# Eight rows of w_gu to a partition, loaded up to 8 MB at a time, with the residual banks holding alternate groups of four columns

## The reference

```
logits = x @ w_router + b_router            # (256, 32); top 4, softmax over the four -> gates
for e in 32 experts:
    h  = x @ w_gu[e] + b_gu[e]              # w_gu[e] is 1024 x 2048: 8 MB
    hg, hu = min(h[:, :1024], 7), clip(h[:, 1024:], -7, 7)
    y  = ((hu + 1) * hg * sigmoid(1.702 * hg)) @ w_down[e] + b_down[e]     # w_down[e] is 1024 x 1024: 4 MB
    out += gate[:, e] * y
```

## Time and profile before

| | |
|---|---|
| median of 3 runs | 1048.63 us |
| the profiled execution's own time | 1049.05 us |
| its span, from first to last instruction | 1047.2 us |
| TensorE matmuls busy | 989.3 us, 94% of the span |
| VectorE busy | 235.0 us, 22% |
| ScalarE busy | 143.3 us, 14% |
| moved by the DMA engines | 421.74 MB, 403 GB/s over the span |
| mean granted TensorE clock | 0.994 of full speed |

### The profile page before, as it was taken

How to read it: one execution, slowest core, us unless ns; L and a number is a source line. 1 busy time by engine, 2 the same in 40 slices (tenths; PEclk the granted TensorE clock), 3 DMA queues, 4 the chain that set the end, 5 groups by cost and what they waited for, 6 DMA issues and landing times.

```text
span 1047.2 us, 12857 instructions
## 1 busy us (share of the span) xinstructions
PE 989.3 (94%) x5782; PEld 413.5 (39%) x5783; DVE 235.0 (22%) x531; ACT 143.3 (14%) x273; POOL 15.9 (2%) x27
## 2 busy tenths in 40 slices
PE   8999999999999999999999999998999889899996
PEld 7875543433333333333333333333333333333332
DVE  3995341111111111111111111101111111011121
ACT  5144320000010101010100010000101000000103
POOL 4000000000000000000000000000000000000001
PEclk9999999999999999999999999999999999999999
DMA  9995489999999999999999999999999999999994
GB/s 307 387 416 196 181 322 409 427 412 427 433 429 431 432 427 426 434 427 432 428 433 427 434 425 437 423 439 423 435 425 433 426 434 429 431 430 430 423 424 165
DMA packets 31220, 421.74 MB, mean 403 GB/s; under 512 B 3791, under 2 KB 8187, under 8 KB 13628
## 3 DMA queue, kind: packets, MB, share of 16 engines
q1 hardware_dynamic: 29612, 420.57, 95.3%
q10 hardware_dynamic: 1552, 0.33, 0.2%
HBM read 419.82 MB, written 1.05 MB: 402 GB/s over the span
## 4 chain that ended last, share of the span: by engine, by line
PE 60%; DMA 25%; DVE 11%; ACT 2%; issue 1%; SPq 0%; POOLq 0%; POOL 0%; DVEq 0%
PE work L1085 52%; DMA ring<-in_w_gu 24%; PE resid L1085 5%; DVE main L821 4%; DVE main L1004 2%; PE work L1405 2%; DVE main L1001 2%; DVE main L997 2%; ACT main L672 1%; DMA ring<-in_w_in 1%; PE work L1201 0%; PE work L1297 0%; DVE main L828 0%; DVE ring L800 0%; DVE ring L831 0%
## 5 line engine op out<-in xcount | busy, mean ns | idle before, releaser
L1085 PE MATMUL work<-ring,main 128*64 128x512 f32 (+1 forms) x3096 | 683.6, 593 | 20.1 <-DMA ring<-in_w_gu 17.8
L1085 PEld LDWEIGHTS work<-ring,main 128*64 128x64 f32 (+1 forms) x3096 | 224.2, 138 | 466.4 <-issue 435.4
L997 DVE TENSOR_SCALAR main<-work 128x512 f32<-128x512 f32 x32 | 22.1, 692 | 738.3 <-PE work L1085 738.3
L672 ACT ACTIVATE main<-main 128x512 f32<-128x512 f32 x32 | 20.2, 631 | 504.0 <-DVE main L997 504.0
L1085 PE MATMUL work<-ring 128*128 128x256 f32 (+2 forms) x308 | 71.9, 403 | 2.1 <-DVE ring L774 0.9
L1085 PE MATMUL resid<-main 128*128 128x512 f32 x128 | 67.6, 613 | 0.9 <-DVE main L1056 0.9
L686 ACT ACTIVATE main<-work 64x512 f32<-64x512 f32 x63 | 37.3, 592 | 215.0 <-PE work L1085 214.6
L1085 PEld LDWEIGHTS work<-ring 128*128 128x128 f32 (+1 forms) x308 | 55.6, 186 | 16.8 <-issue 8.3
L1085 PE MATMUL work<-bgu_rows,ident 128*64 128x512 f32 x256 | 60.8, 594 | 0.0
L1085 PEld LDWEIGHTS work<-select,main 128*128 128x128 bf16 x1536 | 46.6, 98 | 26.2 <-issue 25.2
L1085 PE MATMUL work<-select,main 128*128 128x64 bf16 x1536 | 50.4, 193 | 0.1
(11 more groups left out here) (182 smaller groups left out, 256.0 us busy)
## 6 DMA issues: line engine op xcount, KB each, us to landing
ring<-in_w_gu SPq DMA_DIRECT2D x39, 4096.0 KB, 39.7
ring<-in_w_down SPq DMA_DIRECT2D x20, 4096.0 KB, 39.9
ring<-in_w_gu SPq DMA_DIRECT2D x30, 2048.0 KB, 15.4
ring<-in_w_gu SPq DMA_DIRECT2D x9, 3072.0 KB, 38.2
ring<-in_w_down SPq DMA_DIRECT2D x13, 2048.0 KB, 14.5
ring<-in_w_gu SPq DMA_DIRECT2D x13, 1024.0 KB, 33.2
ring<-in_w_down SPq DMA_DIRECT2D x4, 3072.0 KB, 36.1
ring<-in_w_down SPq DMA_DIRECT2D x9, 1024.0 KB, 28.0
```

The lines of the kernel that those rows point to most:

```text
L672: nc.scalar.activation(sig_h, gate_h, ACT.Sigmoid, scale=SWIGLU_ALPHA).then_inc(sig_ready, 1)
L997: V.tensor_scalar(gate_h, work[:, GATE_BANK, :], SWIGLU_LIMIT, None, ALU.min).then_inc(gate_clamped, 1)
L1085: return nc.tensor.matmul(out_, lhsT, rhs, start=start, stop=stop, skip_group_check=True)
```

## The change

w_gu is laid out with eight neighbouring rows to a partition, one in each up unit, and `UP_GROUP` becomes 8: an expert's eight up units come in one load of 8 MB that reads 64 KB in one run for each partition. Such loads are used from expert 12 on (`HALVES_UP_TO`) to expert 29. Experts before it keep the load sizes that they had (2 units in the first six, then 4), as do experts 30 and 31, but they too have the new row order: a load of 2 units reads 16 KB out of every 64 KB, and one of 4 units reads 32 KB out of every 64 KB. Where a load crosses the end of the ring it is still cut in two.

The rest follows from the row order. A residual bank now holds, of every eight columns, the first four (h = 0) or the last four (h = 1). `project`, `add_bdown` and `down` read their moving operand in groups of four columns with gaps, as `up` did before, and write 512 neighbouring elements. ScalarE copies x into the banks in this order, `gained` reads the final gain and writes the result in groups of four. The gain `norm_ffn_g` comes as one row and is turned by eight small transposes in place of four. Two waits on `o_gained` now ask for both halves, since each multiplication writes into both halves of the result.

```
-    UP_GROUP, DOWN_GROUP = 4, 4
+    UP_GROUP, DOWN_GROUP = 8, 4
-    FINE_UP_TO, FINE_FROM = UNITS * 6, UNITS * (E - 2)
+    FINE_UP_TO, HALVES_UP_TO, FINE_FROM = UNITS * 6, UNITS * 12, UNITS * (E - 2)
-                sizes.append(UP_GROUP if n % UNITS < UP_UNITS else DOWN_GROUP)
+                sizes.append((UP_GROUP if n >= HALVES_UP_TO else UP_GROUP // 2) if n % UNITS < UP_UNITS else DOWN_GROUP)
-        gain_rows = unit(2)[0:2, P:P + 4 * P]
+        gain_rows = unit(2)[0:1, P:P + D]
+        def columns_of(view, h):
+            return view.rearrange("p (j h b) -> p h j b", h=2, b=4)[:, h, :, :]
+        def as_columns(view):
+            return view.rearrange("p (j b) -> p j b", b=4)
-                    g, b = u // 4, u % 4
-                    return w_gu[e, 4 * P * g:4 * P * (g + 1), :].rearrange("(p b) n -> p b n", b=4)[:, b:b + size, :]
+                    return w_gu[e, :, :].rearrange("(p b) n -> p b n", b=KB)[:, u:u + size, :]
...
-                pool.wait_ge(o_gained, h + 1)
+                pool.wait_ge(o_gained, 2)
...
-                nc.scalar.activation(resid[:, t, :], x_sb[:, t, :], ACT.Copy).then_inc(x_added, 1)
+                nc.scalar.activation(resid[:, t, :].rearrange("p (h j b) -> p h j b", h=2, b=4),
+                                     x_sb[:, t, :].rearrange("p (j h b) -> p h j b", h=2, b=4), ACT.Copy).then_inc(x_added, 1)
...
-                V.tensor_tensor(result[:, t, half], resid[:, t, half], final_gain[:, half], ALU.mult).then_inc(o_gained, 1)
+                V.tensor_tensor(columns_of(result[:, t, :], h), as_columns(resid[:, t, half]), columns_of(final_gain, h), ALU.mult)\
+                    .then_inc(o_gained, 1)
...
-                    dve.wait_ge(o_gained, 2 * t + 1)
+                    dve.wait_ge(o_gained, HALVES)
...
-            for b in range(4):
-                last = nc.tensor.transpose(work[:, 3, G_FFN + b:G_FFN + KB:4], gain_rows[:, b:4 * P:4], ident[0:2, 0:2])
+            for b in range(KB):
+                last = nc.tensor.transpose(work[:, 3, G_FFN + b:G_FFN + b + 1], gain_rows[:, b:D:KB], ident[0:1, 0:1])
...
-                    last = mm(resid[:, t, h * HALF:(h + 1) * HALF],
+                    last = mm(as_columns(resid[:, t, h * HALF:(h + 1) * HALF]),
-                              piece(name)[:, kb, h * HALF:(h + 1) * HALF], False, False)
+                              columns_of(piece(name)[:, kb, :], h), False, False)
...
-                            last = mm(work[CAP * h:CAP * (h + 1), UP_BANK if is_last else OUT_BANK, :], lhsT, row[:, h * HALF:(h + 1) * HALF],
+                            last = mm(as_columns(work[CAP * h:CAP * (h + 1), UP_BANK if is_last else OUT_BANK, :]), lhsT, columns_of(row, h),
```

More of the change, by code:

```diff
@@ L186, in hybrid_layer @@
         vec_rows = unit(2)[0:28, 0:P]
-        gain_rows = unit(2)[0:2, P:P + 4 * P]
-        dw_rows = unit(2)[0:TAPS, 5 * P:5 * P + D_CONV]
+        gain_rows = unit(2)[0:1, P:P + D]
+        dw_rows = unit(2)[0:TAPS, P + D:P + D + D_CONV]
         fg = unit(16)[0:HEADS, 0:6 * SEQ].rearrange("p (n t) -> p n t", n=6)
@@ L350, in _ @@
                 at += n
-            sp.dma_start(gain_rows, norm_ffn_g.rearrange("(m q) -> m q", q=4 * P)).then_inc(vecs_in, 16)
+            sp.dma_start(gain_rows, norm_ffn_g.rearrange("(m q) -> m q", q=D)).then_inc(vecs_in, 16)
             sp.dma_start(dw_rows, w_dw).then_inc(dw_in, 16)
@@ L522, in _ @@
             for t in range(TB):
-                nc.scalar.activation(resid[:, t, :], x_sb[:, t, :], ACT.Copy).then_inc(x_added, 1)
-            act.dma_start(wr_sb[:, :, :].rearrange("p (m b) n -> p m (b n)", b=4), w_router.rearrange("(m p b) n -> p m (b n)", p=P, b=4)).then_inc(router_in, 16)
+                nc.scalar.activation(resid[:, t, :].rearrange("p (h j b) -> p h j b", h=2, b=4),
+                                     x_sb[:, t, :].rearrange("p (j h b) -> p h j b", h=2, b=4), ACT.Copy).then_inc(x_added, 1)
+            act.dma_start(wr_sb[:, :, :].rearrange("p b n -> p (b n)"), w_router.rearrange("(p b) n -> p (b n)", b=KB)).then_inc(router_in, 16)
             act.dma_start(br_row[:, :], b_router.partition_broadcast(P)).then_inc(router_in, 16)
@@ L1362, in add_bdown @@
                     for h in range(2):
-                        mm(resid[:, t, h * HALF:(h + 1) * HALF], gates_t[:, t * P:(t + 1) * P], bdown_sb[:, h * HALF:(h + 1) * HALF], False, False)
+                        mm(as_columns(resid[:, t, h * HALF:(h + 1) * HALF]), gates_t[:, t * P:(t + 1) * P], columns_of(bdown_sb, h), False, False)
             def scatter(buffer, t, h, rows=P):
```

## The result

The changed kernel takes 1055.72 us (median of 5 runs, 1055.2 to 1058.64) against 1049.58 us (5 runs): a ratio of 1.0061, with a 95% interval of 1.0047 to 1.0074, or +6.4 us. The forecast of 1051.7 had the sign and was short by 4.0 us. Of these, 0.95 is the kernel before, whose median was 1048.63 when the forecast was made. As a difference, +3.1 was forecast, and +6.1 (by the medians) to +6.4 (by the ratio) was measured; rival A, at +7.0, is nearer.

The account below looks back on a forecast made before the run. The prediction took w_gu[29]'s landing, paced by the DMA, plus 83.9 us behind it as the bound. Terms +6.8 - 3.9 + 0 + 0.2 = +3.1 us on 1048.63 gave 1051.7 us; 8-in-10 range 1048.5 to 1057.0.

Parts of the forecast that it names:

- rival A: DMA loads of w_gu: the large packets save nothing, so the time is 1055.6 us; chance 0.20.
- What bounds the kernel: End of the kernel: landing of the last unit of w_gu[29] plus 83.9 us of TensorE and closing work.
- Point 1: Expert 29's ups: the 8 MB load is waited for whole, 64 instructions behind its landing instead of 32, +6.81 us.
- Point 2: DMA queue: waiting for eight free slots does not run it dry, cost 0; 1 us left for a late load.
- the margin of 7 us: DMA queue at expert 12, the tightest place: at 436 it still has 7 us of work.
- the limit of 0.98: DMA share in 430 to 1000: falling below this anywhere would show the claim of no dry queue wrong.
- Point 3: Experts 12 to 29: one transfer fewer each, 18 x 0.22 = 3.9 us by which w_gu[29] lands earlier.
- The prediction's own sign: Trace of the changed kernel: ten experts take 292.2 us instead of 294.4 if fewer transfers save time.
- the line through two stretches: DMA in 440 to 560 and 963 to 1000: 36.3 ps a byte, 0.027 us a packet, 0.22 us a transfer.
- Point 4: Down product, project, add_bdown and gained in groups of four columns: cost 0, up to 0.7 us in gained.
- Point 5: Start of the kernel: eight transposes for the gain instead of four, +0.2 us, from 0 to 0.6.
- The clock: TensorE's clock may drop after a wait: +1.7 us if it hits expert 29, chance 1 in 5, outside the sum.

Follow-up runs that it names:

- e3: The changed kernel with two 4 MB loads of w_gu for expert 29 alone, 8 MB for experts 12 to 28: 1053.82 us, ratio 1.0034.
- e7: The changed kernel with 4 MB loads of w_gu for experts 26 to 29, 8 MB for experts 12 to 25: 1049.02 us, ratio 0.9991.
- e9: The changed kernel with 4 MB loads of w_gu for experts 28 and 29, 8 MB for experts 12 to 27: 1051.32 us, ratio 1.0017.
- e1: The changed kernel without 8 MB loads of w_gu, its row order, column groups and start kept: 1049.85 us, ratio 0.9995.
- e5: The changed kernel with 8 MB loads of w_gu from expert 6 on in place of 12: 1063.95 us, ratio 1.0137.
- e2: The changed kernel with each 8 MB load sent as two transfers of four units, still waited for together: 1056.91 us, ratio 1.0059.
- e4: The kernel before with 2 MB loads in place of 4 MB everywhere: 1054.05 us, ratio 1.0035.
- e8: The kernel before with 2 MB loads from expert 26 on (before: from expert 30): 1050.58 us, ratio 1.0016.
- e10: The kernel before with one-unit loads for places 24 to 35, where the ring is first refilled, and 20 load semaphores: 1049.76 us, ratio 0.9992.

## Why the prediction was right or wrong

**What bounds the kernel: right.** The landing of w_gu[29] and what TensorE has to do behind it make the end, in this kernel and (with another expert) in e3, e7 and e9, to 0.2 us.

**Point 1, +6.8: right.** The distance from the landing to the end is 90.7 us as forecast; e1, which takes the 8 MB loads away, is back at the kernel before. One sentence in it was too wide, that in the other experts the delay costs nothing. That is true only as long as expert 29 is delayed too. Where expert k is the last with an 8 MB load, the delay costs 6.8 - 2.1 x (29 - k) us, and nothing once this is below 0: 4.7, 2.6 and 0 for e3, e9 and e7. By the ratios they measured 3.6, 1.8 and -0.9, each some 1 us less, with intervals of about 1.3 us to either side. That fits a small saving by the 8 MB loads, but does not prove it.

**Point 2, no dry queue: right,** with the margin of 7 us where it was put. The DMA share of the changed kernel doesn't fall below 0.99 in any stretch of 30 us from 430 to 1000. (In stretches of 10 us it scatters from 0.90 to 1.11 around 1.00, so the limit of 0.98 that the prediction set can't be used there.) e5 shows what lies behind that margin: a queue that loses some 8 us, all of which reaches the end.

**Point 3, -3.9: wrong, and this is the failed term.** The prediction's own sign says so: ten experts took 294.3 us and not 292.2. In its place the runs show about -0.5 us: 0.03 us an expert between e2 and the changed kernel; by the packets of e4 it is 0.02 to 0.07, or 0.4 to 1.3 us in 18 experts. The size is not resolved better than that, and zero is not excluded. The packets did grow as predicted, so "the transfer doesn't do what it says" was not the reason; the other half of rival A was, the line through two stretches took something else for a fixed cost.

A part of what it took is visible in the rows that it used: the SP queue had 100.1% of the engines' time in the earlier trace rows and 99.2% in the earlier trace rows. The line counted the whole stretch as engine time in both. With the shares, 16 x 37 x 0.992 / 902 = 0.651 and 16 x 120 x 1.001 / 1828 = 1.051 us leave 0.012 us a packet and 0.09 a transfer, less than half. That the earlier trace rows is slow for another reason than its packets is shown by the same 37 us in e8:

```profile
DMA packets 1084, 15.79 MB, mean 427 GB/s; under 512 B 120, under 2 KB 120, under 8 KB 120
...
q1 hardware_dynamic: 1082, 15.76, 100.2%
```

These are 962 data packets of 16.4 KB, smaller than the 902 of 17.3 KB, and they carried more.

This correction does not explain the whole miss. Made in the three stretches of 300 us too (100.4, 100.0 and 99.7%), it raises their price, to 0.013 and 0.014 us a packet and 0.11 us a transfer. That agrees with 0.09, and would be 1.6 to 2.0 us in 18 experts. So larger packets did save the engines busy time, but the loads did not land earlier by as much: from 4 MB to 8 MB the queue's share fell from 100.0 to 99.7% and the rate stayed at 430 GB/s. Why it doesn't rise stays open.

The ceiling from the Trainium skill, "DMA: Bandwidth & Descriptors", section "Where 436 GB/s comes from", 435.2 GB/s, was not reached over 300 us: at 39 KB a packet the rate stays at 430. The 1% that is missing does not shrink as the packets grow from 27.7 to 38.7 KB; what it is stays open.

**Point 4, groups of four: right.** The 32 down instructions take 7.09 us, and `gained` 0.69 us as before:

```profile
982.67 7.09 PE L1094 MATMUL work<-ring,main 128*64 128x512 f32 x32
...
1046.03 0.69 DVE L1072 TENSOR_TENSOR main<-resid,ring 128x512 f32<-128x512 f32 x1 [2.89 <-ACT work L510]
```

**Point 5, +0.2: it can't be told.** Expert 0's ups start at 137.40 in the profiled execution for 137.19, which is the 0.2 forecast. But with the start of the kernel before they begin at 136.75 in e10 and 137.79 in e4: single executions differ by more.

**The clock:** no lapse in expert 29 of the profiled execution although it had waited 2.28 us; experts 20, 23 and 27 had one, after 2.63, 2.05 and 2.63 (15.59, 15.65 and 15.35 us for 13.95). There it costs nothing, since the next load is the bound again. e7 and e9 had theirs in just the expert that sets the end, where it cost 1.7 and 1.5 us. Windows of the changed kernel, in the columns of e5's:

```profile
699.80:703.80 4.00, 4.00 (x12) 1.39 (x14) 0.00 (x0) 0.00 (x0) 0.00 (x0) 0.58 1.06 459
703.80:715.40 11.60, 11.60 (x58) 3.92 (x54) 0.00 (x0) 0.00 (x0) 0.00 (x0) 1.00 1.04 452
...
963.96:967.96 4.00, 4.00 (x20) 1.69 (x22) 0.00 (x0) 0.00 (x0) 0.00 (x0) 1.00 0.96 414
```

The sum with point 3 at -0.5 is +6.5, and +6.1 to +6.4 was measured. The time fell into the forecast's range because the range was made wide enough for rival A; the point forecast itself rested on a saving that did not come. Of the 0.65 us by which w_gu[29] landed later in the profiled execution, 0.2 is the start; the rest is less than single executions differ by (963.29 in e2, 964.72 in e1).

## What to carry to other kernels

A larger transfer makes its user wait for all of it. Where transfers set the pace, that moves the work of the whole piece behind the last landing, and the price is paid once, at the end; it is given back by as many iterations with smaller pieces as the delay divided by what the work is faster than the transfers. So load in large pieces in the middle and in small ones towards the end, and look first whether there is anything to be saved: past 28 KB a packet there was 0.1% here at most. When a fixed cost is drawn from two stretches, multiply each by its busy share and take stretches that are long. What comes out is engine time; whether it is also time of the kernel is told by the rate over such stretches, with larger and smaller packets.

## What the runs showed of the hardware

- The rate of the loads is nearly blind to the size of the packets: 427 GB/s at 15.1 KB, 430 at 27.7 and 430 at 38.7, over 300 us each. The share of the engines' time that the queue had fell over the same three, from 100.4 to 100.0 and 99.7%.
- A run of 64 KB for each partition goes as one packet: the mean data packet grew from 28.2 to 39.4 KB when two of 32 KB became one.
- Reading 16 or 32 KB out of every 64 KB of memory costs nothing against 32 KB (e1, ratio 0.9995).
- A DMA queue that lost 8 to 9 us around 270 still sets the end almost 800 us later (e5), while TensorE is full at the time and first waits for a load at 445.
- The clock's lapse after a wait is not a matter of the wait's length alone: none after 2.28 us in the changed kernel and after 3.16 us in e5 (13.95 us for 64 instructions both times), one after 1.97 in e7 (15.65 us) and after 2.02. In the changed kernel a wait of 2.05 us was followed by none at 611.44 (13.95 us, granted clock 1.00 in the first 4 us) and by one at 787.58 (15.65 us, 0.61).
